# The even mixer's seven input units run on activations times scale, with the root applied to their outputs

## The chip, the core and the metric

The kernel runs on one NeuronCore of a Trainium2 chip. Its engines are TensorE (matmuls; PE in the profile), VectorE (DVE), ScalarE (ACT), GpSimd (POOL) and SyncE (SP), which here only issues transfers. SBUF is the working memory; PSUM has 8 banks of 512 float32 columns, written by TensorE. The metric is the device time of one execution in microseconds (us). Before the change it was 1384.68 us, the median of three runs (1384.54 to 1387.13).

## The reference, cut to what matters

One step of a two-layer trunk over 384 tokens: 128 context tokens and 256 latent ones, 1024 channels, each with its own shift, scale and gate per sub-layer. A layer is feed-forward, mixer, feed-forward. Each sub-layer reads a modulated RMS norm:

```python
def modulate(x, g, shift, scale):
    return rms_norm(x, g) * (1 + scale) + shift

def even_mixer(h, w_in, w_out, ...):
    q, k, v, a = jnp.split(h @ w_in, [ATT_Q, ATT_Q + ATT_KV, ATT_Q + 2 * ATT_KV], axis=-1)
    q = rms_norm(q.reshape(bsz, length, N_HEADS, HEAD_DIM), q_g)
    k = rms_norm(k.reshape(bsz, length, N_KV_HEADS, HEAD_DIM), k_g)
    ...                                   # latent tokens: rotary; cached keys and values put ahead
    glu = a[..., :CONV_CH] * jax.nn.sigmoid(a[..., CONV_CH:])
    conv = jax.nn.silu(layer_norm(depthwise_conv(glu, conv_w, conv_b), cn_g, cn_b))   # 31 taps, 512 channels
    return jnp.concatenate([attn, conv], axis=-1) @ w_out
```

The projection h @ w_in has 14 column tiles of 128: 4 of queries, 1 of keys, 1 of values, 4 + 4 of the gated product.

## The kernel before, in words

Activations lie with channels on the partitions and tokens along the free dimension: x is 8 tiles of 128 channels by 384 tokens. All big products are made in three parts, high and low halves of weights and activations (three(), lines 1417 to 1421). A weight unit is 128 x 2048 float32, two column tiles over 8 row tiles; SyncE loads it (L416) into one of four slots when the unit four places before is done, ScalarE makes its high half (split, L594), VectorE the low one (split, L904), and TensorE runs its 48 matmuls (in_unit). Each engine's order is the order of its block in the file; semaphores tie them.

The mixer has 7 input units: unit 0 is the first pair of gated-product tiles, unit 1 keys and values, 2 and 3 the queries, 4 to 6 the other gated-product pairs; then 4 output units. Ahead of it come feed-forward 0's last unit, whose 8 output tiles VectorE adds to x one by one (L963). ScalarE squares each (L610), TensorE sums over channels and spreads the inverse root to all partitions (norm_sums, norm_spread, with dummy matmuls, L1527, between), VectorE and ScalarE make the scaled, shifted high and low parts (L982, L620, L990), and first_unit follows them tile by tile.

The other boundaries, into the two feed-forwards behind and into the odd mixer, work differently (raw_boundary, raw_norm, raw_units): TensorE multiplies x times scale (xt_hi, xt_lo) with two further columns that hold the shifts, 386 in all, at once for two units, the sums and the spread of the root stand inside, and the outputs are multiplied by the root (n_rms) and get the shift's product added when they are read.

In the mixer, VectorE also has the convolution of channel tiles 0 and 2, one instruction per tap (taps, L1182, 399 columns); tiles 1 and 3 go to TensorE as 8 "quads" each (conv_quads_of, L1716), from copies that SyncE makes by 16 small transfers a tile (L504) as soon as the gated product of that tile is in padded (glu_mul, L1193). The gated product of tile j needs ScalarE's sigmoid j. ScalarE evicts keys, values and queries from PSUM (qkv_evict); VectorE rotates (L1225 to L1234).

The attention has 12 steps m, a pair of heads and 128 tokens each. In step m TensorE runs the scores of m+2, its quads, the values of m-1 and the transposes (flip) of m; ScalarE the exp of m and copies; VectorE a reciprocal (L1260), a scaling (L1265), the maxima of m+1 (L1253) and some taps. After it come the output units, with the convolution's layer norm beside them.

## Time and profile before

| | |
|---|---|
| median of 3 runs | 1384.68 us |
| profiled execution | 1386.83 us, its span 1385.0 us |
| TensorE matmul busy | 1368.4 us, 99% |
| VectorE busy | 972.3 us, 70% |
| ScalarE busy | 552.5 us, 40% |
| GpSimd busy | 47.8 us, 3% |
| mean granted TensorE clock | 0.995 |

The span is from the first to the last instruction of the profiled execution; times in rows are us from its start. A matmul of 384 columns shows 0.34 us although a new one goes out every 0.17, since their ends overlap: the distance between starts is what counts. A value in brackets is the idle time of that engine before the instruction and who ended it. The granted clock is 1.00 at 2.4 GHz and 0.50 at 1.2 GHz.

### The profile page before, as it was taken

To read this page: it belongs to the slowest core of one execution; us is meant where nothing else is said; L and a number is where in the kernel's file an instruction comes from. 1 tells how busy PE (TensorE), PEld (TensorE's weight loads), DVE (VectorE), ACT (ScalarE), POOL (GpSimd) and SP (SyncE) were. 2 spreads that over 40 slices of the span, in tenths; PEclk is the share of its full clock that TensorE was granted. 3 is DMA by queue.
4 is the path that set the end of the run, shared out by engine and by line. 5 is a ranking of instruction groups with operands and counts; after the bars stand their busy time and mean duration, and the time that the engine had idled before them with its cause. 6 is when DMAs were issued, how large, how long until landed. Compare 5 with 4: busy or idle time off the path is not lost.

```text
span 1385.0 us, 21119 instructions
## 1 busy us (share of the span) xinstructions
PE 1368.4 (99%) x8065; PEld 1331.5 (96%) x8065; DVE 972.3 (70%) x1474; ACT 552.5 (40%) x758; POOL 47.8 (3%) x50
## 2 busy tenths in 40 slices
PE   7999999999999999999999999999999999999999
PEld 6999999999948999999999999999998999999999
DVE  5698889948885988888339888888386588443522
ACT  4433333235476643333226433332274463333320
POOL 0000000011001200000002000000020100000000
PEclk8999999999999999999999999999999999999999
DMA  9766567533411465564334666665334253333331
...
DMA packets 48758, 245.65 MB, mean 177 GB/s; under 512 B 6336, under 2 KB 10688, under 8 KB 28096
## 3 DMA queue, kind: packets, MB, share of 16 engines
...
q8 instruction: 34, 0.56, 0.2%
q14 instruction: 20, 0.16, 0.0%
q10 hardware_dynamic: 288, 0.13, 0.0%
HBM read 240.80 MB, written 1.70 MB: 175 GB/s over the span
## 4 chain that ended last, share of the span: by engine, by line
PE 96%; DVE 2%; DMA 1%; ACT 1%; SPq 0%; issue 0%; DVEq 0%; ACTq 0%
PE ps L1419 30%; PE ps L1421 30%; PE ps L1420 30%; DMA m_raw<-in_w_pairs 1%; PE ps L1825 1%; PE ps L1827 1%; PE ps L1826 1%; PE ps L1480 0%; DVE conv L1182 0%; PE ps L1754 0%; PE ps L1496 0%; PE ps L1716 0%; PE ps L1728 0%; DVE smax L1253 0%; PE ps L1854 0%; PE ps L1743 0%
## 5 line engine op out<-in xcount | busy, mean ns | idle before, releaser
L1419 PE MATMUL ps<-a_hi,w_hi 128*128 128x384 f32 x1552 | 522.3, 337 | 0.5 <-DVE a_lo L990 0.3
L1420 PE MATMUL ps<-a_lo,w_hi 128*128 128x384 f32 x1552 | 519.3, 335 | 0.0
L1421 PE MATMUL ps<-a_hi,w_lo 128*128 128x384 f32 x1552 | 519.2, 335 | 0.0
L904 DVE TENSOR_TENSOR w_lo<-w_raw,w_hi 128x2048 fp32r<-128x2048 f32 x153 | 352.0, 2302 | 176.9 <-ACT w_hi L594 176.8
L594 ACT ACTIVATE w_hi<-w_raw 128x2048 fp32r<-128x2048 f32 x153 | 291.7, 1910 | 247.3 <-DMA w_raw<-in_w_units 247.1
L926 DVE SCALAR_TENSOR_TENSOR m_raw<-m_raw 128x1024 f32<-128x1024 f32 x256 | 299.2, 1218 | 0.0
L1419 PEld LDWEIGHTS ps<-a_hi,w_hi 128*128 128x128 f32 x1552 | 291.8, 188 | 6.6 <-issue 3.4
L1420 PEld LDWEIGHTS ps<-a_lo,w_hi 128*128 128x128 f32 x1552 | 291.9, 188 | 0.1
L1421 PEld LDWEIGHTS ps<-a_hi,w_lo 128*128 128x128 f32 x1552 | 291.8, 188 | 0.0
L1421 PE MATMUL ps<-h_hi,w_lo 128*128 (+1 forms) x704 | 235.2, 334 | 0.0
L1419 PE MATMUL ps<-h_hi,w_hi 128*128 (+1 forms) x704 | 235.2, 334 | 0.0
L1420 PE MATMUL ps<-h_lo,w_hi 128*128 (+1 forms) x704 | 235.2, 334 | 0.0
L673 ACT ACTIVATE glu<-ps 128x384 f32<-128x384 f32 x82 | 40.0, 488 | 279.9 <-PE ps L1421 279.9
L1419 PEld LDWEIGHTS ps<-h_hi,w_hi 128*128 128x128 f32 x704 | 132.1, 188 | 0.0
L1420 PEld LDWEIGHTS ps<-h_lo,w_hi 128*128 128x128 f32 x704 | 132.1, 188 | 0.0
L1421 PEld LDWEIGHTS ps<-h_hi,w_lo 128*128 128x128 f32 x704 | 132.1, 188 | 0.0
L1069 DVE TENSOR_TENSOR glu<-glu,ps 128x384 f32<-128x384 f32 x82 | 45.0, 549 | 75.0 <-ACT glu L673 75.0
L675 ACT ACTIVATE h_hi<-glu 128x384 f32 (+1 forms) x82 | 43.1, 525 | 132.6 <-DVE glu L1069 132.6
L1072 DVE TENSOR_TENSOR h_lo<-glu,h_hi 128x384 f32 (+1 forms) x82 | 45.8, 558 | 66.5 <-ACT h_hi L675 66.5
L620 ACT ACTIVATE a_hi<-n_full,m_shift 128x128 fp32r<-128x128 f32 x96 | 42.3, 455 | 45.2 <-DVE n_full L982 45.2
L963 DVE SCALAR_TENSOR_TENSOR x<-ps,m_gate,x 128x128 f32<-128x128 f32 x96 | 34.7, 412 | 26.5 <-PE ps L1421 26.2
L1419 PE MATMUL ps<-xt_hi,w_hi 128*128 128x386 f32 x128 | 44.2, 345 | 0.1
...
## 6 DMA issues: line engine op xcount, KB each, us to landing
...
m_raw<-in_w_rows SPq DMA_DIRECT2D x128, 512.0 KB, 5.5
...
```

What stands on the lines that cost most here:

```text
L594: nc.scalar.activation(w_hi[:, slot(u), :], w_raw[:, slot(u), :], ACT.Copy).then_inc(hi_done, 1)
L620: nc.scalar.activation(a_hi[:, d, lo:hi], n_full[:, d, lo:hi], ACT.Identity, bias=m_shift[:, n, d, cnd:cnd + 1]).then_inc(a_hi_done, 1)
L673: nc.scalar.activation(glu[:, 0, :], ps[:, 2 * b, 0:TOK], ACT.Silu).then_inc(silu_done, 1)
L675: nc.scalar.activation(h_hi[:, bass.ds(t + RING * i, 1), :], glu[:], ACT.Copy).then_inc(h_hi_done, 1)
L904: nc.vector.tensor_tensor(w_lo[:, slot(u), :], w_raw[:, slot(u), :], w_hi[:, slot(u), :].bitcast(FP32), ALU.subtract).then_inc(lo_done, 1)
L926: nc.vector.scalar_tensor_tensor(out, mod_rows(n % TRING), 1.0, cond_row(cnd), ALU.mult, ALU.mult, accum_out=mod_cols[:, bass.ds(FIRST_TIL ...
L963: ins = nc.vector.scalar_tensor_tensor(x[:, d, lo:hi], ps[:, d, lo:hi], m_gate[:, s, d, cnd:cnd + 1], x[:, d, lo:hi], ALU.mult, ALU.add)
L1069: nc.vector.tensor_tensor(glu[:, 0, :], glu[:, 0, :], ps[:, 2 * b + 1, 0:TOK], ALU.mult).then_inc(prod_done, 1)
L1072: nc.vector.tensor_tensor(h_lo[:, bass.ds(t + RING * i, 1), :], glu[:], h_hi[:, bass.ds(t + RING * i, 1), :].bitcast(FP32), ALU.subtract). ...
L1419: mm(out, whi, mhi, start=start, stop=False)
L1420: mm(out, whi, mlo, start=False, stop=False)
L1421: return mm(out, wlo, mhi, start=False, stop=stop)
```

## The change

The mixer's seven input units take the form of the other boundaries. Units 0 and 1 run as raw_units on x times scale, held in a_hi and a_lo (widened to 400 columns); units 2 to 6 read the same 386 columns with in_unit. There is no normed copy of x for the mixer any more, and norm_sums, norm_spread with the dummies, and first_unit are gone. VectorE has a new step take(n) per unit: it copies the shift columns out of PSUM, for keys and queries also times their gain, and multiplies both tiles of the unit (768 columns) by n_rms into SBUF; TensorE may use those banks again after it (in_scaled). ScalarE then works from SBUF with the shift as bias, in two pieces (context and latent tokens) where it had one. The units use banks 0, 2, 4, 0, 2, 4, 2. The transpose of the new keys moves into unit 6. Tile 0's taps are spread anew; all of tile 2's taps stand in the attention's steps, 3 each in steps 0 to 8 and 2 in steps 9 and 10, where 7 stood ahead and then 3, 3, 3, seven times 2, and 1. The first quads go ahead of the second scores. VectorE's split of unit 8 stands behind the attention.

```diff
+    return (a_hi, a_lo) if n == 1 else (xt_hi, xt_lo)
+def glu_pair(j):
+    return prob_t if j % 2 else prob
...
-    norm(1)
+    raw_norm(1, UNIT0[1])
     u = UNIT0[1]
     def sigmoid(n, j):
-        act.wait_ge(unit_done, RING + u + n + 1)
+        act.wait_ge(in_scaled, n + 1)
         if j >= 2:
             act.wait_ge(glu_done, j - 1)
-        nc.scalar.activation(e_sig[:, j % 2, :], ps[:, GLU_BANK[j] + 1, 0:TOK], ACT.Sigmoid).then_inc(sig_done, 1)
+        for cnd, lo, hi in SEGS:
+            ins = nc.scalar.activation(e_sig[:, j % 2, lo:hi], glu_pair(j)[:, 1, lo:hi], ACT.Sigmoid,
+                                       bias=in_shift[:, n, 1, cnd:cnd + 1])
+        ins.then_inc(sig_done, 1)
...
-        act.wait_ge(unit_done, RING + u + n + 1)
+        act.wait_ge(in_scaled, n + 1)
         for h in range(2):
-            m = 2 * (n - 1) + h
-            tile = (QT, None, 0, 1, 2, 3)[m]
-            dst = v_raw[:] if tile is None else qk[:, tile, :]
-            src = ps[:, QKV_BANK[n] + h, 0:TOK]
-            if tile is not None:
-                nc.scalar.activation(qk_sq[:, tile, :], src, ACT.Square).then_inc(qk_sq_done, 1)
-            if tile is None:
-                nc.scalar.activation(dst, src, ACT.Copy).then_inc(qk_copied, 1)
-            else:
-                col = B_KG if tile == QT else B_QG
-                nc.scalar.activation(dst, src, ACT.Copy, scale=vec_b[:, col:col + 1]).then_inc(qk_copied, 1)
-    split(u + 2)
-    split(u + 3)
+            tile = (QT, QT + 1, 0, 1, 2, 3)[2 * (n - 1) + h]
+            if tile <= QT:
+                for cnd, lo, hi in SEGS:
+                    ins = nc.scalar.activation(qk_sq[:, tile, lo:hi], qk[:, tile, lo:hi], ACT.Square,
+                                               bias=in_shift[:, n, h, cnd:cnd + 1])
+                ins.then_inc(qk_sq_done, 1)
+            col = B_KG if tile == QT else B_QG
+            for cnd, lo, hi in SEGS:
+                if tile > QT:
+                    ins = nc.scalar.activation(qk[:, tile, lo:hi], qk[:, tile, lo:hi], ACT.Identity,
+                                               bias=in_shift[:, n, h, cnd:cnd + 1])
+                else:
+                    ins = nc.scalar.activation(qk[:, tile, lo:hi], qk[:, tile, lo:hi], ACT.Identity,
+                                               bias=in_shift_g[:, n - 1, h, cnd:cnd + 1], scale=vec_b[:, col:col + 1])
+            ins.then_inc(qk_copied, 1)
     sigmoid(0, 0)
     split(u + 4)
     qkv_evict(1)
...
-    inverse_rms(1)
-    norm(1)
     u = UNIT0[1]
     tap_at = {}
+    def take(n):
+        bank = IN_BANK[n]
+        dve.wait_ge(unit_done, RING + u + n + 1)
+        dve.wait_ge(rms_copied, 1)
+        shifts = ps[:, bank:bank + 2, TOK:TOK + 2]
+        nc.vector.tensor_copy(in_shift[:, n], shifts)
+        if n in QKV_UNITS:
+            col = B_KG if n == 1 else B_QG
+            nc.vector.tensor_scalar(in_shift_g[:, n - 1], shifts, vec_b[:, col:col + 1], None, ALU.mult)
+            dst = qk[:, (QT, 0, 2)[n - 1]:(QT, 0, 2)[n - 1] + 2, :]
+        else:
+            dst = glu_pair(GLU_UNIT.index(n))[:]
+        nc.vector.tensor_tensor(dst, ps[:, bank:bank + 2, 0:TOK], n_rms[:].unsqueeze(1).to_broadcast([P, 2, TOK]),
+                                ALU.mult).then_inc(in_scaled, 1)
     def taps(j, k0, k1):
...
                 ins.then_inc(conv_done, 1)
     def glu_mul(j):
+        n = GLU_UNIT[j]
+        dve.wait_ge(in_scaled, n + 1)
         dve.wait_ge(sig_done, j + 1)
         dve.wait_ge(e_zero, 1)
         for sgm, lo, hi in SEGS:
-            ins = nc.vector.tensor_tensor(padded[:, j, PAD_AT[sgm]:PAD_AT[sgm] + hi - lo],
-                                          e_sig[:, j % 2, lo:hi], ps[:, GLU_BANK[j], lo:hi], ALU.mult)
+            ins = nc.vector.scalar_tensor_tensor(padded[:, j, PAD_AT[sgm]:PAD_AT[sgm] + hi - lo],
+                                                 glu_pair(j)[:, 0, lo:hi], in_shift[:, n, 0, sgm:sgm + 1],
+                                                 e_sig[:, j % 2, lo:hi], ALU.add, ALU.mult)
         ins.then_inc(glu_done, 1)
     split(u + 2)
-    glu_mul(0)
     split(u + 3)
     dve.wait_ge(vectors_in, 48)
+    take(0)
+    take(1)
+    split(u + 4)
+    glu_mul(0)
     dve.wait_ge(glu_done, 1)
     taps(0, 0, 5)
-    split(u + 4)
-    taps(0, 5, 16)
+    take(2)
     split(u + 5)
-    taps(0, 16, 24)
+    taps(0, 5, 13)
+    take(3)
     split(u + 6)
-    taps(0, 24, 28)
+    taps(0, 13, 20)
     NS = 2 * TT * (QT + 1)
     dve.wait_ge(qk_stat, 1)
     nc.vector.tensor_scalar(stat[:, 0:NS], ps[:, 6, 0:NS], 1.0 / HD, RMS_EPS, ALU.mult, ALU.add).then_inc(qk_ms, 1)
-    taps(0, 28, 30)
+    taps(0, 20, 23)
     dve.wait_ge(qk_root, 1)
     dve.wait_ge(dve_self, mark(nc.vector.reciprocal(stat_row[:, 0:NS], stat_row[:, 0:NS])))
     nc.vector.tensor_copy(qk_wide[:], stat_row[:, 2 * TT * QT:NS].unsqueeze(2).to_broadcast([P, 2 * TT, HD])
                           ).then_inc(qk_wide_done, 1)
-    taps(0, 30, CONV_K)
+    taps(0, 23, 25)
+    take(4)
     split(u + 7)
     glu_mul(1)
     dve.wait_ge(glu_done, 2)
...
     dve.wait_ge(qk_bc, 1)
     dve.wait_ge(roped, 1)
     nc.vector.tensor_tensor(qk[:, QT, :], qk[:, QT, :], ps[:, BC_BANK_K, 0:TOK], ALU.mult).then_inc(k_roped, 1)
+    take(5)
+    taps(0, 25, 28)
     glu_mul(2)
+    taps(0, 28, CONV_K)
     def attention(m):
         width = CTX if m % TT == 0 else LAT + PAST
...
     def mix_low(j, src):
         dve.wait_ge(mix_hi, j + 1)
-        nc.vector.tensor_tensor(a_lo[:, j, :], src, a_hi[:, j, :].bitcast(FP32), ALU.subtract).then_inc(mix_ready, 1)
-    split(u + 8)
-    dve.wait_ge(glu_done, 3)
-    taps(2, 0, 7)
+        nc.vector.tensor_tensor(a_lo[:, j, 0:TOK], src, a_hi[:, j, 0:TOK].bitcast(FP32), ALU.subtract).then_inc(mix_ready, 1)
+    take(6)
+    attention(0)
     glu_mul(3)
-    attention(0)
     attention(1)
     dve.wait_ge(glu_done, CT)
     for m in range(PAIR_STEPS):
...
             mix_low((m - 4) // TT, ps[:, 0, 0:TOK])
         if 1 <= m < PAIR_STEPS - 1:
             attention(m + 1)
-        k = 7 + 2 * m + min(m, 3)
-        taps(2, min(k, CONV_K), min(k + 2 + (m < 3), CONV_K))
+        k = 2 * m + min(m, 9)
+        taps(2, min(k, CONV_K), min(k + 2 + (m < 9), CONV_K))
         if m == PAIR_STEPS - 2:
             dve.wait_ge(conv_done, DVE_TILES)
             a = mark(nc.vector.tensor_tensor(conv_sum(), conv[:, 0, :], conv[:, 2, :], ALU.add))
...
     dve.wait_ge(quad_out, 2)
     nc.vector.tensor_tensor(conv_sum(), conv_sum(), conv[:, 3, :], ALU.add).then_inc(conv_summed, 1)
     mix_low(QT - 1, ps[:, 0, 0:TOK])
+    split(u + 8)
...
     ffn(0)
-    norm(1)
     u = UNIT0[1]
-    first_unit(u, GLU_BANK[0], 1)
-    in_unit(u + 1, QKV_BANK[1])
-    in_unit(u + 2, QKV_BANK[2])
+    raw_units(u, 1)
+    in_unit(u + 2, IN_BANK[2], cols=TOK + 2)
...
         ins.then_inc(qk_bc, 1)
     pe.wait_ge(e_zero, 4)
+    pe.wait_ge(in_scaled, 1)
     qk_sums(QT)
     cached_and_values()
-    pe.wait_ge(glu_done, 1)
-    in_unit(u + 3, QKV_BANK[3])
+    in_unit(u + 3, IN_BANK[3], cols=TOK + 2)
     qk_sums(0)
     qk_sums(1)
-    in_unit(u + 4, GLU_BANK[1], 0, {3: last_sums})
-    in_unit(u + 5, GLU_BANK[2], 0, {3: spread_keys})
-    pe.wait_ge(k_roped, 1)
-    pe.wait_ge(glu_done, 2)
-    nc.tensor.transpose(ps[:, 3, 0:P], qk[:, QT, 0:CTX], ident[:]).then_inc(e_t, 1)
+    pe.wait_ge(in_scaled, 2)
+    in_unit(u + 4, IN_BANK[4], 0, {6: last_sums}, cols=TOK + 2)
+    pe.wait_ge(in_scaled, 3)
+    in_unit(u + 5, IN_BANK[5], 0, {3: spread_keys}, cols=TOK + 2)
+    def keys_out():
+        pe.wait_ge(k_roped, 1)
+        nc.tensor.transpose(ps[:, 0, 0:P], qk[:, QT, 0:CTX], ident[:]).then_inc(e_t, 1)
+    pe.wait_ge(in_scaled, 5)
+    in_unit(u + 6, IN_BANK[6], 0, {6: keys_out}, cols=TOK + 2)
     pe.wait_ge(qk_ms, 1)
-    in_unit(u + 6, GLU_BANK[3])
     pe.wait_ge(glu_done, 3)
     pe.wait_ge(roped, 1)
...
         ins.then_inc(pv_done, 1)
     scores(0)
+    conv_quads_of(QUADS_AT[0])
+    pe.wait_ge(in_scaled, 7)
     scores(1)
-    conv_quads_of(QUADS_AT[0])
     for m in range(PAIR_STEPS):
...
 DFT_BANK = [2, 0, 3]
-GLU_BANK = [0, 2, 4, 6]
-QKV_BANK = {1: 2, 2: 4, 3: 0}
+IN_BANK = [0, 2, 4, 0, 2, 4, 2]
+GLU_UNIT, QKV_UNITS = [0, 4, 5, 6], (1, 2, 3)
 BC_BANK_K = 7
```

VectorE, from unit 4's split (the first row) on; padded is the gated product, conv the taps, w_lo a split. Before:

```order
L904 TENSOR_TENSOR w_lo<-w_raw,w_hi 128x2048
L1182 SCALAR_TENSOR_TENSOR conv<-padded,conv_wt,conv 128x399 x11
L904 TENSOR_TENSOR w_lo<-w_raw,w_hi 128x2048
L1182 SCALAR_TENSOR_TENSOR conv<-padded,conv_wt,conv 128x399 x8
L904 TENSOR_TENSOR w_lo<-w_raw,w_hi 128x2048
L1182 SCALAR_TENSOR_TENSOR conv<-padded,conv_wt,conv 128x399 x4
L1212 TENSOR_SCALAR stat<-ps 128x30
L1182 SCALAR_TENSOR_TENSOR conv<-padded,conv_wt,conv 128x399 x2
L1215 RECIPROCAL stat_row<-stat_row 128x30
```

and now, from the same split:

```order
L909 TENSOR_TENSOR w_lo<-w_raw,w_hi 128x2048
L1206 SCALAR_TENSOR_TENSOR padded<-prob,in_shift,e_sig 128x128
L1206 SCALAR_TENSOR_TENSOR padded<-prob,in_shift,e_sig 128x256
L1189 TENSOR_SCALAR conv<-padded,conv_wt,vec_b 128x399
L1193 SCALAR_TENSOR_TENSOR conv<-padded,conv_wt,conv 128x399 x4
L1175 COPY in_shift<-ps 128x4
L1178 TENSOR_SCALAR in_shift_g<-ps,vec_b 128x4
L1182 TENSOR_TENSOR qk<-ps,n_rms 128x768
L909 TENSOR_TENSOR w_lo<-w_raw,w_hi 128x2048
L1193 SCALAR_TENSOR_TENSOR conv<-padded,conv_wt,conv 128x399 x8
L1175 COPY in_shift<-ps 128x4
L1178 TENSOR_SCALAR in_shift_g<-ps,vec_b 128x4
```

The first gated product and its first five taps now come behind that split, and a take (in_shift, in_shift_g, qk<-ps,n_rms) stands ahead of each further one.

VectorE, from the second gated product on, before (rot and qk<-m_raw are the rotation, L1245 the product that ends the keys):

```order
L1193 TENSOR_TENSOR padded<-e_sig,ps 128x128
L1193 TENSOR_TENSOR padded<-e_sig,ps 128x256
L1225 TENSOR_TENSOR rot<-qk,rope 128x1280
L1230 TENSOR_TENSOR qk<-m_raw,rope 128x5x256
L1234 TENSOR_TENSOR qk<-qk,rot 128x5x256
L1245 TENSOR_TENSOR qk<-qk,ps 128x384
L1193 TENSOR_TENSOR padded<-e_sig,ps 128x128
L1193 TENSOR_TENSOR padded<-e_sig,ps 128x256
L904 TENSOR_TENSOR w_lo<-w_raw,w_hi 128x2048
L1178 TENSOR_SCALAR conv<-padded,conv_wt,vec_b 128x399
L1182 SCALAR_TENSOR_TENSOR conv<-padded,conv_wt,conv 128x399 x6
```

and now, from the take of unit 5, behind the same keys' product, to the first scores' maxima:

```order
L1175 COPY in_shift<-ps 128x4
L1182 TENSOR_TENSOR prob<-ps,n_rms 128x768
L1193 SCALAR_TENSOR_TENSOR conv<-padded,conv_wt,conv 128x399 x3
L1206 SCALAR_TENSOR_TENSOR padded<-prob,in_shift,e_sig 128x128
L1206 SCALAR_TENSOR_TENSOR padded<-prob,in_shift,e_sig 128x256
L1193 SCALAR_TENSOR_TENSOR conv<-padded,conv_wt,conv 128x399 x3
L1175 COPY in_shift<-ps 128x4
L1182 TENSOR_TENSOR prob_t<-ps,n_rms 128x768
L1274 TENSOR_REDUCE smax<-ps 128x2
L1276 SCALAR_TENSOR_TENSOR smaxn<-smax,stat_row 128x2
L1206 SCALAR_TENSOR_TENSOR padded<-prob_t,in_shift,e_sig 128x128
L1206 SCALAR_TENSOR_TENSOR padded<-prob_t,in_shift,e_sig 128x256
```

Two takes are new; the split has gone from here, and tile 0's last six taps stand where tile 2's first seven did.

TensorE, from the last matmul of unit 6 into the attention (L1728 scores, L1716 quads), before:

```order
L1421 MATMUL ps<-a_hi,w_lo 128x384
L1728 MATMUL ps<-kdup,qk 128x128 x2
L1728 MATMUL ps<-kdup,qk 128x384 x2
L1716 MATMUL ps<-m_raw 32x399 x16
L1728 MATMUL ps<-kdup,qk 128x384 x2
L1716 MATMUL ps<-m_raw 32x399 x4
L1743 MATMUL ps<-ident,prob 128x128 x2
L1728 MATMUL ps<-kdup,qk 128x128 x2
```

and now (L1725 scores, L1713 quads):

```order
L1441 MATMUL ps<-a_hi,w_lo 128x386
L1725 MATMUL ps<-kdup,qk 128x128 x2
L1713 MATMUL ps<-m_raw 32x399 x16
L1725 MATMUL ps<-kdup,qk 128x384 x4
L1713 MATMUL ps<-m_raw 32x399 x4
L1740 MATMUL ps<-ident,prob 128x128 x2
L1725 MATMUL ps<-kdup,qk 128x128 x2
```

The 16 quad matmuls now stand between the first scores and the second.

## Rows read from the trace of the kernel before

**Rows 1.** TensorE in order of time: start, duration, line, operation, tiles, forms, [idle before <-releaser].
```profile
308.42 0.34 PE L1421 MATMUL ps<-h_hi,w_lo 128*128 128x384 f32 x1
...
315.48 0.42 PE L1419 MATMUL ps<-a_hi,w_hi 128*128 128x384 f32 x1
```

**Rows 2.** Windows: stretch, length, each engine's busy us, granted clock, DMA share, GB/s.
```profile
311.90:315.20 3.30, 3.30 (x15) 3.30 (x16) 1.70 (x5) 0.91 (x2) 0.00 (x0) 0.50 0.28 117
18.30:28.40 10.10, 8.89 (x51) 6.25 (x52) 7.19 (x17) 3.71 (x5) 0.00 (x0) 0.50 1.02 422
395.00:400.00 5.00, 2.98 (x24) 1.63 (x26) 4.29 (x12) 4.49 (x14) 0.00 (x0) 1.00 0.00 2
```

**Rows 3.** TensorE in order of time, between the second and third feed-forward.
```profile
734.89 0.34 PE L1419 MATMUL ps<-xt_hi,w_hi 128*128 128x386 f32 x1
...
739.10 0.75 PE L1496 MATMUL ps<-ones,n_acc 128*128 128x1 f32 x6
...
753.14 0.34 PE L1419 MATMUL ps<-a_hi,w_hi 128*128 128x384 f32 x1
```

**Rows 4.** TensorE in order of time: after the third input unit, and at the attention.
```profile
342.46 0.72 PE L1661 MATMUL ps<-pick_half,qk_sq 128*128 128x2 f32 x6
...
380.50 1.14 PE L1728 MATMUL ps<-kdup,qk 64*128 64x128 f32 x8
381.57 2.89 PE L1716 MATMUL ps<-m_raw 128*32 128x399 f32 x32
```

**Rows 5.** VectorE in order of time, even mixer and (last) the third feed-forward.
```profile
345.83 2.28 DVE L904 TENSOR_TENSOR w_lo<-w_raw,w_hi 128x2048 fp32r<-128x2048 f32 x1
348.03 5.32 DVE L1182 SCALAR_TENSOR_TENSOR conv<-padded,conv_wt,conv 128x399 f32<-128x399 f32 x8
...
363.65 0.62 DVE L1193 TENSOR_TENSOR padded<-e_sig,ps 128x128 f32<-128x128 f32 x2 [0.82 <-ACT e_sig L719]
...
368.95 0.55 DVE L1245 TENSOR_TENSOR qk<-qk,ps 128x384 f32<-128x384 f32 x1
...
757.70 1.01 DVE L1048 TENSOR_TENSOR n_sq<-ps,n_rms 128x384 f32<-128x384 f32 x2
```

**Rows 6.** ScalarE in order of time.
```profile
318.63 0.90 ACT L620 ACTIVATE a_hi<-n_full,m_shift 128x128 fp32r<-128x128 f32 x2 [0.41 <-DVE n_full L982]
...
330.73 1.92 ACT L594 ACTIVATE w_hi<-w_raw 128x2048 fp32r<-128x2048 f32 x1 [1.86 <-DMA w_raw<-in_w_units]
```

**Rows 7.** SyncE in order of time, and landing of the issues of L504, 360 to 380.
```profile
364.30 11.32 SPq L504 DMA_DIRECT2D m_raw<-padded  x16
...
DMA to landing us min/median/max: 1.9/2.2/4.0
```

**Rows 8.** VectorE in order of time, attention.
```profile
383.60 0.17 DVE L1260 RECIPROCAL srec<-ssum 128x2 f32<-128x2 f32 x1 [0.25 <-ACT prob L801]
...
386.42 0.95 DVE L1253 TENSOR_REDUCE smax<-ps 128x2 f32<-128x768 f32 x1
...
405.26 0.17 DVE L1260 RECIPROCAL srec<-ssum 128x2 f32<-128x2 f32 x1 [1.25 <-ACT e_sig L801]
...
409.12 0.17 DVE L1260 RECIPROCAL srec<-ssum 128x2 f32<-128x2 f32 x1 [0.27 <-ACT prob L801]
...
414.74 0.17 DVE L1260 RECIPROCAL srec<-ssum 128x2 f32<-128x2 f32 x1 [0.58 <-ACT prob L801]
...
418.80 0.16 DVE L1260 RECIPROCAL srec<-ssum 128x2 f32<-128x2 f32 x1
```

**Rows 9.** Chain of waits: start, duration, work on the chain.
```profile
420.26 0.49 PE ps L1743 x3
...
421.76 0.88 PE ps L1754 x12
...
434.03 0.56 PE ps L1790 x6
```

**Rows 10.** GpSimd in order of time.
```profile
427.58 5.18 POOL L571 TENSOR_TENSOR qk_sq<-qk_sq 128x384 f32<-128x384 f32 x3 [96.34 <-ACT qk_sq L822]
```

162 lines of the change are left out of this document (65 added, 97 removed).

## The prediction

> **What bounds the kernel now.** I read the page's first part, then TensorE's rows in order of time at the start of the even mixer, then the windows with the granted clock, and last VectorE's, ScalarE's and SyncE's rows beside them. TensorE is busy 99% of the span (the table above), so a change pays only where TensorE has no full-size matmul to do. In the part that is edited there are two such places.
>
> The first is the seam between the first feed-forward and the mixer. The last of its matmuls is issued at 308.42, the next full one at 315.48 [rows 1]; between them stand sums, a root, a spread and dummies, all serial. I take the end of the feed-forward as 308.6. The third input unit is done by 342.46, where the small sums start [rows 4], so three units and the seam take 33.9 us. The granted clock is 0.50 from 311.9 to 315.2, the 1.2 GHz level [rows 2]; its cost is part of the 33.9.
>
> The second is the attention. It starts with the scores at 380.50 [rows 4] and ends with the last value products, at 421.76 plus 0.88 [rows 9]. Its twelve steps are a relay of VectorE (maxima, reciprocals, taps of the convolution), ScalarE (exp) and TensorE. VectorE is nearly full: it idles only 0.27 us before three of its reciprocals (the one at 409.12 stands for them), 1.25 before that at 405.26 and 0.58 before that at 414.74 [rows 8]. What is added to VectorE here is therefore mostly paid.
>
> **The seam.** The new form runs units 0 and 1 on x times scale, with the root taken meanwhile. The same code already stands between the second and third feed-forward: its first matmul is at 734.89, and the next kind begins at 753.14, 18.25 us for two units with sums and spread inside, and no wait [rows 3]. The residual additions ahead of it run at the same distance from the seam in both places, and the parameters are ready before them, so I take 18.25 here too: units 0 and 1 end at 308.6 + 18.25 = 326.85. A matmul of 386 columns goes out every 0.175 us (24 of them from 734.89 to 739.10) [rows 3], a unit is 48 of them, 8.4 us. Unit 2 ends at 335.3 instead of 342.5: 7.2 us earlier. Vector work for the norm (32 scaled and low parts) goes, 16 raw low parts come, none of it late.
>
> **Units 3 to 6.** Before, from 342.46 to 380.50 it is 38.0 us of units and small matmuls without a wait [rows 4]. Two columns in 384 add 0.5%, 0.2 us. New waits could stand in it. Values must be copied before their transposes: VectorE takes unit 1 by about 328.2, ScalarE splits unit 4 at 330.73 as before [rows 6] (its load is released by unit 0 in both, at about 326) and is done 332.65, then three pairs of activations of 0.8 to 0.9 each [rows 6] end at 335.2, and TensorE arrives at 335.9. The transpose of the new keys needs the roped keys; they come 5.9 us after the second gated product starts (363.65 to 369.50) [rows 5], in the new order at about 368.4, and TensorE is at its place in unit 6 at 371. I charge nothing; each cover is 0.7 us or more. The units end at 335.3 + 38.2 = 373.5, 7.0 us earlier.
>
> **Where it is given back: the quads' transfers.** The second convolution tile goes by 16 small transfers to TensorE. They are issued on SyncE after the second gated product (glu_done 2), and before took 364.30 to 375.62 to issue, the last started 10.7 after the first and landing a median 2.2 later [rows 7]. Before, TensorE reached the quads at 381.57 [rows 4] and never felt them. When is that product ready now? VectorE's program from ScalarE's 332.65 on: four splits of 2.20 (345.83 to 348.03), 25 taps of 0.655 (eight are 5.3 us) = 16.3, two gated products of 0.65 [rows 5], three statistics operations 0.75 together, and three new "take" steps. A take reads two banks, 768 columns, times the root, and copies the shifts. No row has it: from below 0.5 (the 384-column one, two in 1.01 [rows 5]), from above two such, 1.1 with the copies; a pitch of 0.46 for 384 columns makes 768 nearer the upper end, and I take 1.0 to 1.1. Together 8.8 + 16.3 + 1.3 + 0.75 + 3.2 = 30.35: the product is ready at 363.0, only 1.3 earlier than before. VectorE stays the pace although TensorE gained 7: it stands idle from about 328.2 to 332.65, and then does the same taps and more. The last transfer starts at 373.7 and lands at 375.9.
>
> The new TensorE order is scores(0), four quads (2.9 us [rows 4]), scores(1). Scores(0) is done at 374.0; TensorE stands until 375.9, the quads end at 378.8, scores(1) 0.85 later, and VectorE's maximum over 768 columns and its scaling (0.95 and 0.1 [rows 8]) at 381.0. Take 6, which sits behind three taps and ends at 375.1, is covered by that; so is ScalarE's last sigmoid with the table load, which leave exp(0) at 378.2. The first reciprocal now stands behind the second maximum, at 381.1; before it was at 383.60 [rows 8]. So 2.5 us remain of the 7.0.
>
> **The taps in the attention.** All 31 taps of the other vector tile now stand in the steps; before 7 of them were done ahead. Steps 0 to 2 keep three taps; steps 3 to 8 get a third one, step 10 a second: 7 x 0.655 = 4.6 us. The idle time that can take them is 3 x 0.27 + 1.25 + 0.58 = 2.6 [rows 8], so the last reciprocal is about 1.9 us later relative to the start. The last reciprocal has some 0.9 us to spare: it and its scaling are over at 419.4 (418.80 and 0.6 [rows 8]), and the flips that need them are released by other work and run at 420.26 [rows 9]. So 1.1 us reaches the end. Bounds: 0 (all hidden) and 4.6 (none).
>
> **After it.** The split of unit 8 moves from before the attention to its end, 2.2 us ahead of the layer norm, which waits for TensorE's means anyway, so it starts only some 0.65 later. GpSimd's three additions follow, 427.58 to 432.76 [rows 10], and TensorE uses them at 434.03 [rows 9], so 0.65 still fits. Everything later keeps its distance.
>
> **Sum.** -2.5 + 1.1 = -1.4 us. The profiled execution is 1386.83 us (span 1385.0 and 1.8 around it) and would become 1385.4; it lies 2.15 above the median of the runs, 1384.68, and the runs' time becomes 1383.3.
>
> **Rivals.** (a) The transfers don't hold TensorE: they issue faster (without the long issues among them) and the product is ready sooner. For it: nothing in the trace ever waited for them. Against it: 11.3 us for 16 is what stands there [rows 7]. Then the start is bounded by take 6 at 375.1, exp(0) at 378.2 and the second maximum, first reciprocal at 378.4, 5.2 earlier: -5.2 + 1.1 = -4.1, 1380.6. Halfway is possible. (b) The taps are paid in full, because a later maximum delays exp, the flips and the next maximum in turn: -2.5 + 4.6 = +2.1, 1386.8. For it: in steps 0 to 3, which have three taps already, the chain of waits runs through VectorE alone. Against it: from step 5 to 10 it runs through TensorE and ScalarE. (c) Slower: TensorE's clock. The new stand of 1.9 us before the quads has no instruction in it. The clock fell to 1.2 GHz at 18.3, after a thin stretch from 14.6, and at 311.9, after the 3.3 us since the last full matmul; it stayed low for 10.1 us and for 3.3 [rows 2]. If it falls at about 376 for 10 us, the quads and scores(1) cost 3.65 us more and two steps of some 3 us of TensorE work lose about a microsecond each: -1.4 + 5 = +3.6, 1388.3. It decides from the point where the transfers land so late that the stand resembles the stretches ahead of those two falls; I reckon it shorter. Against it: in 395 to 400 TensorE was busy 2.98 of 5 us and the clock stayed at 1.00 [rows 2]. ("TensorE: Matmul & The Clock Gate" of the Trainium skill, section on the HAM clock gate, says that idling brings half the clock and that activity releases it; by that rule the old seam's fall belongs to what the change removes, and the trace agrees with the 0.50 in it, and the new stand is where it could return.)
>
> **Chances.** Forecast 0.48, (a) or most of it 0.28, (b) 0.13, (c) 0.11. Its own range is 1381.8 to 1385.0 (product and landing 0.8 either way, taps 0 to 2). To hold 8 in 10 I reach down past (a) to 1379.8 and up to (b) at 1386.8. A measurement tells 0.2% (2.8 us) from no change: faster, below 1381.9, is (a) and a sixth of the forecast, 0.36; slower, above 1387.5, is (c) and a part of (b), 0.14; the rest 0.50.
>
> **What will show it.** In the changed profile: no small matmuls between feed-forward and mixer, 18.2 us for units 0 and 1, clock 1.00; the units ending near 373.5; 16 transfers from 363; a stand of about 2 us of TensorE before the quads, released by a transfer; first reciprocal at 381; VectorE without idle time in steps 3 to 8; attention ending about 421.2 instead of 422.6. The forecast is wrong if TensorE's quads start straight behind scores(0), if a unit waits for a take, or if the clock falls in the attention.

## Result and profile after

The changed kernel takes 1391.09 us (median of 12 runs, 1388.05 to 1394.51), the kernel before, beside it, 1385.18 (12 runs, 1384.36 to 1388.84): ratio 1.0037, 95% interval 1.0029 to 1.0044. It is 5.1 us slower by the ratio and 5.9 by the medians. The forecast was 1383.3, with 1386.8 as the upper end. The profiled executions differ by 4.8: 1391.61 us with a span of 1389.8, against 1385.0 (the table of before). What follows accounts for these 4.8.

The seam went as forecast, and so did most of the mixer. TensorE in order of time in the changed kernel; the rows answer [rows 1, 4, 9] and, from 464 on, the start of the sums (ones, n_acc) and of the spread (ident, stat) at the next boundaries:

```profile
309.05 0.33 PE L1441 MATMUL ps<-h_hi,w_lo 128*128 128x384 f32 x1
309.23 0.34 PE L1439 MATMUL ps<-a_hi,w_hi 128*128 128x386 f32 x1
...
313.44 0.75 PE L1506 MATMUL ps<-ones,n_acc 128*128 128x1 f32 x6
...
335.93 0.72 PE L1654 MATMUL ps<-pick_half,qk_sq 128*128 128x2 f32 x6
...
374.34 0.49 PE L1725 MATMUL ps<-kdup,qk 64*128 64x128 f32 x4
376.69 4.58 PE L1713 MATMUL ps<-m_raw 128*32 128x399 f32 x32 [1.85 <-DMA m_raw<-padded]
381.20 1.56 PE L1725 MATMUL ps<-kdup,qk 64*128 64x384 f32 x8
...
422.21 0.88 PE L1751 MATMUL ps<-prob_t,v_nat 128*64 128x128 f32 x12 [0.69 <-ACT prob_t L796]
...
437.20 0.83 PE L1796 MATMUL ps<-e_diag,ones 128*128 128x128 f32 x6
...
464.34 0.83 PE L1506 MATMUL ps<-ones,n_acc 128*128 128x1 f32 x6 [1.02 <-POOL n_acc L550]
...
467.24 0.83 PE L1479 MATMUL ps<-ident,stat 128*128 128x128 f32 x6
...
741.34 0.83 PE L1506 MATMUL ps<-ones,n_acc 128*128 128x1 f32 x6
```

The mixer's first matmul follows the feed-forward's last one by 0.18 us, where there were 7 us before. The small sums behind unit 2 come at 335.93 instead of 342.46, the attention at 374.34 instead of 380.50. Then the quads stand 1.85 us for their transfers and take 4.58 us instead of 2.89. The attention ends at 422.21 + 0.88, where it ended at 421.76 + 0.88 before. The feed-forward ahead of the mixer ends at 309.2 in this profile, not at 308.6; against that offset of 0.6 the mixer up to the attention's end is 0.15 us faster and no more.

The granted clock at the quads, in windows (columns as in [rows 2]):

```profile
376.00:377.00 1.00, 0.31 (x4) 0.16 (x8) 0.56 (x3) 0.88 (x3) 0.00 (x0) 0.92 0.72 134
377.00:380.00 3.00, 3.00 (x24) 0.96 (x20) 0.75 (x2) 2.28 (x6) 0.00 (x0) 0.50 0.96 380
380.00:381.00 1.00, 1.00 (x16) 0.26 (x8) 0.00 (x0) 0.00 (x0) 0.00 (x0) 0.88 0.98 377
```

A clock of 0.92 in the first window, 0.50 in the second and 0.88 in the third make 3.4 us at 1.2 GHz. The fall comes just behind the stand, and the quads take 1.7 us longer by it. VectorE, answering [rows 5, 8]:

```profile
333.99 2.29 DVE L909 TENSOR_TENSOR w_lo<-w_raw,w_hi 128x2048 fp32r<-128x2048 f32 x1 [4.88 <-ACT w_hi L600]
...
363.39 0.74 DVE L1206 SCALAR_TENSOR_TENSOR padded<-prob_t,in_shift,e_sig 128x128 f32<-128x128 f32 x2
...
375.12 0.95 DVE L1182 TENSOR_TENSOR prob_t<-ps,n_rms 128x768 f32<-128x768 f32 x1
...
382.16 0.96 DVE L1274 TENSOR_REDUCE smax<-ps 128x2 f32<-128x768 f32 x1 [4.42 <-PE ps L1725]
...
383.23 0.17 DVE L1281 RECIPROCAL srec<-ssum 128x2 f32<-128x2 f32 x1
...
419.79 0.16 DVE L1281 RECIPROCAL srec<-ssum 128x2 f32<-128x2 f32 x1
```

VectorE stands 4.88 us for unit 4's split (it waits for ScalarE's half) and 4.42 for the second scores. The second gated product ends at 364.1 (forecast 363.0), the 16 transfers go out from 364.16 to 375.24 (before 364.30 to 375.62 [rows 7]).

The loss lies behind the mixer, and a little of it ahead. In the table are stage lengths, each the difference of two row starts as above; "end of mixer" is from the last small matmuls of the layer norm (e_diag) to the sums of the next boundary, the others from a spread to the next sums, the last to the end of the span. With the tiles 384 columns apart such a stage repeats to 0.1 us from profile to profile of the same program. With 400 columns the odd mixer does not: it takes 93.07 to 93.14 us in three of the six profiles that have it, this one among them, and 92.65 in the other three. The 0.45 us lie among the last 24 matmuls ahead of the next sums, and what decides on them is not shown. The second feed-forward has 0.2 us more here than in the other five (273.89 to 273.90).

| us | before | after | difference |
|---|---|---|---|
| start to the end of the first feed-forward | 308.6 | 309.2 | +0.6 |
| from there to e_diag | 128.0 | 128.0 | 0.0 |
| end of mixer | 26.21 | 27.14 | +0.93 |
| second feed-forward | 273.37 | 274.10 | +0.73 |
| third | 273.58 | 273.89 | +0.31 |
| odd mixer | 91.49 | 93.14 | +1.65 |
| fourth | 272.35 | 272.93 | +0.58 |

These sum to 4.8 us, the difference of the spans (the four boundaries' own 2.8 to 2.9 us each differ by 0.1 at most). No instruction of the last four rows computes anything else than before. Two things around them are different: the tiles of a_hi and a_lo lie 400 columns apart, and the program ahead has other instructions and another number of them.

### The profile page after: what moved, and what is told of

Its sections match the earlier page's. It is cut to its first block, busy times and chain, and to the rows that moved or that the text cites. A ratio compares the mean times of both kernels' runs of the same rounds, so it can differ in the third digit from the quotient of the medians.

```text
span 1389.8 us, 21090 instructions
## 1 busy us (share of the span) xinstructions
PE 1369.2 (99%) x8037; PEld 1332.0 (96%) x8037; DVE 977.0 (70%) x1476; ACT 556.2 (40%) x774; POOL 49.5 (4%) x52
## 4 chain that ended last, share of the span: by engine, by line
PE 67%; DVE 3%; issue 2%; SPq 1%; POOL 1%; ACT 0%; DMA 0%; DVEq 0%; POOLq 0%; ACTq 0%
PE ps L1439 21%; PE ps L1441 21%; PE ps L1440 21%; DVE conv L1193 1%; PE ps L1824 1%; PE ps L1823 1%; PE ps L1825 1%; SPq L511 1%; DVE smax L1274 1%; POOL n_acc L550 1%; PE ps L1713 0%; PE ps L1852 0%; PE ps L1506 0%; PE ps L1843 0%; PE ps L1479 0%
## 5 line engine op out<-in xcount | busy, mean ns | idle before, releaser
L1439 PE MATMUL ps<-a_hi,w_hi 128*128 128x384 f32 (+1 forms) x1552 | 524.7, 338 | 0.1
L1440 PE MATMUL ps<-a_lo,w_hi 128*128 128x384 f32 (+1 forms) x1552 | 521.9, 336 | 0.0
L1441 PE MATMUL ps<-a_hi,w_lo 128*128 128x384 f32 (+1 forms) x1552 | 521.8, 336 | 0.0
L619 ACT ACTIVATE a_hi<-n_full,m_shift 128x128 fp32r<-128x128 f32 x80 | 35.4, 455 | 39.7 <-DVE n_full L987 39.6
```

The costliest lines, as they stand in the source:

```text
L619: nc.scalar.activation(a_hi[:, d, lo:hi], n_full[:, d, lo:hi], ACT.Identity, bias=m_shift[:, n, d, cnd:cnd + 1]).then_inc(a_hi_done, 1)
L1439: mm(out, whi, mhi, start=start, stop=False)
L1440: mm(out, whi, mlo, start=False, stop=False)
L1441: return mm(out, wlo, mhi, start=False, stop=stop)
```

## Experiments

Each time measured below is the median of 5 to 12 executions, and its ratio is to the kernel before, run beside it, whose median lay between 1385.68 and 1386.12. The kernels' code is shortened below. A trace is one execution, up to 2.6 us from its kernel's median.

**The distance of the tiles.** First the kernel before with wide tiles of which it reads the same 384 columns (XT_N is 400):

```diff
-a_hi = sb("a_hi", [P, KT, TOK], F32R)        # and a_lo
+a_hi = sb("a_hi", [P, KT, XT_N], F32R)[:, :, 0:TOK]
```

> The kernel before, with one edit: the tiles of a_hi and a_lo lie 400 columns apart in SBUF instead of 384; every instruction reads and writes the same 384 columns as before. Theory W (the distance of the tiles): the changed kernel's matmuls on a_hi and a_lo are issued irregularly and about 0.0005 us further apart in the feed-forwards (0.1733 before, 0.1738 to 0.1739 after), 0.005 in the odd mixer's row units; over some 4,600 of the first and 150 of the second that is 2.3 + 0.8 = 3 us: 1388.2, ratio 1.002. Theory R (the place): all that lies behind a_lo has moved by 1024 bytes, and that is what counts: also 1388.2. Theory T (timing alone: what is lost after the mixer comes from loads and additions that start later, not from the layout): 1385.2, ratio 1.000, and an unchanged distance of the matmuls.

Measured: 1389.6 us, ratio 1.0028 (1.0017 to 1.0038). Then the kernel before with unused memory behind the two tiles instead:

```diff
 a_lo = sb("a_lo", [P, KT, TOK], F32R)
+sb("a_room", [P, 2 * KT * (XT_N - TOK)], F32R)
```

> The kernel before, with one edit: 1024 unused bytes per partition behind a_lo, so that all that lies behind it has the address of the changed kernel, while the tiles of a_hi and a_lo stay 384 columns apart. Theory W: no change, 1385.2. Theory R: 1388.2, as with the wide tiles. Theory T: no change, 1385.2.

Measured: 1386.23, ratio 1.0002 (0.9993 to 1.0011). TensorE's spread and the next sums around the second feed-forward and around the odd mixer, first with the wide tiles, then with the room:

```profile
467.96 0.83 PE L1470 MATMUL ps<-ident,stat 128*128 128x128 f32 x6
...
741.85 0.75 PE L1497 MATMUL ps<-ones,n_acc 128*128 128x1 f32 x6
...
1021.65 0.83 PE L1470 MATMUL ps<-ident,stat 128*128 128x128 f32 x6
...
1114.72 0.73 PE L1497 MATMUL ps<-ones,n_acc 128*128 128x1 f32 x6
```

```profile
465.78 0.83 PE L1470 MATMUL ps<-ident,stat 128*128 128x128 f32 x6
...
739.14 0.75 PE L1497 MATMUL ps<-ones,n_acc 128*128 128x1 f32 x6
...
1018.43 0.83 PE L1470 MATMUL ps<-ident,stat 128*128 128x128 f32 x6
...
1109.93 0.72 PE L1497 MATMUL ps<-ones,n_acc 128*128 128x1 f32 x6
```

273.89 and 93.07 us against 273.36 and 91.50. The same instructions on the same data take 0.5 us more per feed-forward and 1.6 in the odd mixer (0.4 of them are the wait named above, so 1.2 for the matmuls), only because the tiles are further apart; moving what lies behind them by 1024 bytes costs nothing that the interval can show. Theory W stands, R and T fall. The first feed-forward, whose start differs from profile to profile, says the same behind it: from 86.04 us (its 201st matmul that reads a_hi) to 217.08 (the first that reads h_hi) it is 131.04 us before, and so in all seven profiles with tiles 384 apart; in all six with 400 it is 131.47. What follows there reads h_hi and h_lo, whose tiles have not moved, and takes 91.35 in both. In the changed kernel the wide form is needed only by the seven input units, so the rest can keep its own view of the same memory:

```diff
+a_hi, a_lo = first KT * TOK columns of each, as [P, KT, TOK]     # feed-forwards, output units, odd mixer
+xa_hi, xa_lo = all KT * XT_N columns, as [P, KT, XT_N]           # raw_pair(1), in_unit with 386 columns
```

(in words, not code)

> The changed kernel, with one edit: the seven input units still read 386 columns of tiles 400 apart, but everything else (feed-forwards, output units, odd mixer) lays its tiles 384 apart in the same memory. Addresses behind a_lo are those of the changed kernel. Theory W: 3 us less than the changed kernel, 1388.1, ratio to the kernel before 1.002; what then remains of the 5.9 us is the mixer and its seam to the third sub-layer (1.5 us in the traces). Theory R or T: as the changed kernel, 1391.1, ratio 1.004.

Measured: 1387.88, ratio 1.0020 (1.0010 to 1.0030), and in its trace the feed-forwards are 273.47, 273.37 and 272.45 us, the odd mixer 91.49: what the distance costs is back in these stages. The ratio gains only 0.0017, 2.4 us, since its profile loses 1.4 us elsewhere, at the boundary ahead of the second feed-forward (under "The instruction fetch").

Two more runs ask what it is about the distance that costs, both in the kernel before:

```diff
+sb("a_shift", [P, 16], F32R)
 a_hi, a_lo as before                    # distance 384, begin 64 bytes later
```

> The kernel before, with one edit: a_hi and a_lo begin 64 bytes later, their tiles still 384 columns (1536 bytes) apart; what lies behind them is 1024 bytes later as in the run with the room, which cost nothing. It asks what about the distance of 1600 bytes costs. Theory A (where a tile begins: 1600 bytes put every second tile on an address that is no multiple of 128 bytes, and here all are): the cost is there in full or double, 1389 to 1393, and the matmuls on a_hi show 337 to 339 ns instead of 336. Rival D (the distance itself, not where a tile begins): 1386, and 336, 334, 334 ns as before.

```diff
-a_hi = sb("a_hi", [P, KT, TOK], F32R)        # and a_lo
+a_hi = sb("a_hi", [P, KT, 416], F32R)[:, :, 0:TOK]     # 1664 bytes, 13 x 128
```

> The kernel before, with one edit: the tiles of a_hi and a_lo are 416 columns (1664 bytes, 13 x 128) apart, 32 unused columns in each where the distance of 400 has 16. Theory A (a tile that begins off a multiple of 128 bytes costs): no cost, 1386, 336, 334, 334 ns. Rival D (any distance other than that of the tiles' own width costs) : 1389 to 1390, as with 400. A finer rule, with multiples of 256 or 512 bytes wanted, would also show a cost here and in part of the tiles.

Measured: with the shift 1387.02, ratio 1.0007 (0.9998 to 1.0016); with 416 1394.53, ratio 1.0064 (1.0050 to 1.0077). By stages:

| us | second, third feed-forward | odd mixer | of it a_hi, a_lo stationary | moving | fourth |
|---|---|---|---|---|---|
| 384 | 273.37, 273.58 | 91.49 | 32.90 | 33.31 | 272.35 |
| 384, 64 bytes later | 273.38, 273.60 | 92.38 | 33.81 | 33.29 | 272.45 |
| 400 | 273.89, 274.09 | 93.07 | 33.60 | 33.78 | 272.88 |
| 416 | 274.97, 275.19 | 92.61 | 33.60 | 33.71 | 274.00 |

A matmul holds one operand, the stationary one, and runs the other, the moving one, through it. The two new columns are from the first to the last start of the odd mixer's 144 matmuls with a_hi or a_lo as the stationary operand (in pieces of 128 columns) and of its 192 with them as the moving one. In the feed-forwards they are the moving operand.

Theory A fails where it was meant: in the feed-forwards the shift costs nothing and 416 costs three times what 400 does, 1.6 us each, though no tile's begin has moved against a multiple of 128 bytes. There the distance itself counts; rival D had the kind right, but gave 416 the price of 400. With the tiles as the stationary operand it is otherwise: the shift alone costs 0.9, and 400 and 416 cost 0.7 each. Why a matmul is issued later when its neighbour tile is further away no run shows.

**The order at the attention's start.**

```diff
 scores(0)
-conv_quads_of(QUADS_AT[0])
 pe.wait_ge(in_scaled, 7)
 scores(1)
+conv_quads_of(QUADS_AT[0])
```

> The changed kernel, with one edit: the second scores stand ahead of the first quads again, as before the change. The unit's outputs are taken at 376.1 in the changed kernel's trace, so the second scores can go there; the second maximum then starts at about 378 instead of 382.2, the first reciprocal at 379 instead of 383.2. Theory V (VectorE sets the pace of the steps, and the stand of TensorE ahead of the quads was the loss): the attention ends 3 to 4 us earlier, 1387.5. Theory Q (the four quads only move into the relay: they run at half clock behind the second scores and delay the third scores and the first flip): gain 0 to 1, 1390.5.

Measured: 1388.41, ratio 1.0022 (1.0010 to 1.0034), 2.1 us better than the changed kernel by the ratios, where theory V had 3 to 4. Its executions lie between 1385.74 and 1393.99, and the profiled one, 1387.12, is among the faster. VectorE there (the first scores start 0.5 earlier than in the changed kernel's profile):

```profile
377.25 0.95 DVE L1274 TENSOR_REDUCE smax<-ps 128x2 f32<-128x768 f32 x1
...
378.98 0.17 DVE L1281 RECIPROCAL srec<-ssum 128x2 f32<-128x2 f32 x1 [0.58 <-ACT prob L806]
```

The first reciprocal is 4.25 us earlier and the attention ends at 417.96 instead of 422.21, just as much: 3.8 us without the offset. The 16 quad matmuls, now behind 0.92 us of scores, take 2.89, so a part of the 3.8 is the clock, at most the 1.7 that the quads had lost, and the rest is the order. Theory V stands in the trace.

**The stand and the clock.** Nine dummy matmuls (2.27 us), whose results nobody reads, in the place of the stand, in the changed kernel:

```diff
 scores(0)
+for _ in range(9):
+    mm(ps[:, IDLE_BANK, 0:128], ones[:], ident[:, 0:128], start=True, stop=True)
 conv_quads_of(QUADS_AT[0])
```

> The changed kernel, with one edit: nine dummy matmuls (128 x 128, 36 instructions) between the first scores and the first quads, where TensorE stood 1.85 us for the quads' transfers. Theory C (the stand itself costs the clock): the granted clock stays 1.00 from 376 to 381, the 16 quad matmuls take 2.9 us instead of 4.58, the first reciprocal and the end of the attention come 1.7 us earlier. Rival: the clock falls all the same, since the thin stretch is longer than the stand, and nothing changes there. Theory F (instruction fetch): the q8 packet of 16 KB, one per some 256 TensorE instructions, lay 2.5 us behind the issue of a weight load in the changed kernel (444.75 against 442.28) and 0.6 us ahead of it in the kernel before (441.0 against 441.68), and the load took 5.9 us instead of 4.6; 36 instructions more put the fetch 3 us earlier, the load takes 4.7 again, and TensorE's wait of 1.0 us for GpSimd's sums ahead of the third sub-layer is gone. C and F together: -2.7 us, 1388.4; C alone -1.7, F alone -1.0.

Measured: 1389.89, ratio 1.0031 (1.0022 to 1.0040): 0.8 us better by the ratios, where both theories together have 2.7, and not told apart from none by the intervals. The profiled execution, 1387.78, is among the faster, and the slower ones have a lower mean clock (0.994 at 1392 and 1393 us, 0.997 in the profiled one), so the clock fell somewhere in them too; where, no profile shows. The profiled one is plain on both theories.

```profile
373.81 2.27 PE L1758 MATMUL ps<-ident,ones 128*128 128x128 f32 x18
376.01 2.89 PE L1713 MATMUL ps<-m_raw 128*32 128x399 f32 x32
```

The granted clock is 1.00 throughout, the quads take 2.89 instead of 4.58, and from the first scores to the second maximum it is 6.4 us instead of 7.8. So the stand itself had brought the clock down: the granted clock fell at the quads in the three profiles with a stand of 1.82 us or more there and in none of the others. Part is given back ahead of it: in this trace TensorE waits 0.77 us for ScalarE's copies of the values, since unit 4's load lands 6.5 us behind its issue, not 5.4 (more on that load below).

**The instruction fetch.** What made the end of the mixer 0.93 us longer? ScalarE's third split there waits for its load in the changed kernel and does not in the kernel before:

```profile
448.24 1.92 ACT L600 ACTIVATE w_hi<-w_raw 128x2048 fp32r<-128x2048 f32 x1 [1.17 <-DMA w_raw<-in_w_units]
```

That load of 1 MB is issued at 442.28 and lands 5.9 us later; before it was issued at 441.68 and took 4.6. Nothing else is loaded then, but for one packet of 16 KB on the queue for instructions (q8). Such packets come every 15 to 23 us in the mixer; inside each feed-forward there is a stretch of 153 to 158 us without one. Nine dummies of 16 columns in the opening, far ahead, move it:

```diff
 keep_busy(BUSY_OPENING)
+for _ in range(9):
+    mm(ps[:, IDLE_BANK, 0:16], ones[:], ident[:, 0:16], start=True, stop=True)
```

> The changed kernel, with one edit: nine dummy matmuls of 16 columns more (36 instructions) in the opening, behind the 22 that stand there, where TensorE waits for parameter loads. This moves only the instruction fetches. Theory F: the load takes 4.7 us instead of 5.9, ScalarE's third split doesn't wait, TensorE's wait of 1.0 us for GpSimd ahead of the third sub-layer is gone, and the kernel is 1.0 us faster, 1390.1, if no other load is hit instead. Rival B (the load is late for another reason, the second set of quad transfers or the later split of unit 8): load 5.9, wait 1.0, 1391.1. The quads' stand and the clock at 376 to 381 stay as they were.

Measured: 1390.1, ratio 1.0025 (1.0014 to 1.0036), 1.7 us better than the changed kernel by the ratios, with overlapping intervals; the trace decides. Queue packets from 444.75 to 445.00 and the load's landing (issue, KB, median us) in the changed kernel:

```profile
q8 instruction: 1, 0.02, 23.5%
...
w_raw<-in_w_units SPq DMA_DIRECT2D x1, 1024.0 KB, 5.9
```

With the dummies in the opening, packets from 441.75 to 442.00, and the same load, issued at 442.26:

```profile
q8 instruction: 1, 0.02, 29.9%
...
w_raw<-in_w_units SPq DMA_DIRECT2D x1, 1024.0 KB, 4.7
```

The packet came 2.5 us behind the issue and comes 0.4 ahead of it now. The load is back at 4.7 us, TensorE's wait for GpSimd is gone, and the end of the mixer takes 26.41 instead of 27.14 (the 0.2 that remains is the distance: the wide kernel before has 26.39). Theory F stands, B falls. The packet is TensorE's, since only its instructions were added. All nine profiles of kernels with the change agree: in the five with the changed kernel's count of TensorE instructions the packet comes 2.5 to 3.0 us behind the issue and the load takes 5.9 to 6.1, in the four with nine dummies more it comes at the issue or up to 0.5 ahead of it and the load takes 4.7 to 4.8. How the packet holds the load up isn't shown. In the kernel with the two views the same wait (1.31 us) was followed by a granted clock of 0.57 from 464 to 468, and the boundary took 4.3 us instead of 2.9.

**VectorE's stand ahead of the transfers.** In the changed kernel:

```diff
 sigmoid(0, 0)                    # ScalarE
-split(u + 4)
 qkv_evict(1)
+split(u + 4)
...
 take(1)                          # VectorE
-split(u + 4)
 glu_mul(0)
 taps(0, 0, 5)
+split(u + 4)
```

> The changed kernel, with one edit: unit 4's split goes behind the keys' and values' activations on ScalarE, and behind the first gated product and its five taps on VectorE, which otherwise stands 4.9 us for that split from 329.1 on. It tests the step of the forecast by which the quads' transfers hold TensorE because VectorE stands idle there. Theory S: the second gated product comes some 3 us earlier (360 instead of 363.4), the last transfer lands before the first scores are done, TensorE does not stand ahead of the quads, the granted clock stays 1.00, and with 1.85 us of stand and 1.7 of slow matmuls gone the second maximum starts at about 379 instead of 382.2: 2.5 to 3.5 us faster, 1388. Rival: the time is taken up by the next wait (the take of unit 4 or the sigmoid), and 0 to 1 us is gained.

Measured: 1388.82, ratio 1.0021 (1.0012 to 1.0030), 2.2 us better than the changed kernel by the ratios.

```profile
374.44 0.88 PE L1713 MATMUL ps<-m_raw 128*32 128x399 f32 x8 [1.50 <-DMA m_raw<-padded]
...
377.26 1.56 PE L1725 MATMUL ps<-kdup,qk 64*128 64x384 f32 x8
```

VectorE at the splits of units 4 and 5 and at the second gated product:

```profile
334.08 2.29 DVE L909 TENSOR_TENSOR w_lo<-w_raw,w_hi 128x2048 fp32r<-128x2048 f32 x1 [3.00 <-ACT w_hi L600]
...
338.84 2.29 DVE L909 TENSOR_TENSOR w_lo<-w_raw,w_hi 128x2048 fp32r<-128x2048 f32 x1 [1.40 <-ACT w_hi L600]
...
361.13 0.74 DVE L1206 SCALAR_TENSOR_TENSOR padded<-prob_t,in_shift,e_sig 128x128 f32<-128x128 f32 x2
```

The sequence starts 1.9 us earlier in this profile (unit 2's sums at 334.04 against 335.93), so the gated product is only 0.4 earlier beside it (361.13 against 363.39), not 3. VectorE did its other work ahead of the split, but stood 3.00 us for unit 4's split and then 1.40 for unit 5's, 4.4 in all where it was 4.88. Unit 4's load landed 7.4 us behind its issue, not 5.4. Unit 5's load, issued 3.5 us behind it, and the two copies of the keys, issued at 328.98 and 329.75 here and at 335.55 and 336.17 in the changed kernel, lie within its time; no run has them apart. The transfers still hold TensorE 1.5 us; yet here the clock did not fall at the quads, and the second maximum is 2.0 us earlier beside the rest. So both were half right: the stand stays, the slow matmuls went.

**Together.** Views and the second scores first:

> The changed kernel with both edits that gained: tiles 384 apart outside the seven input units, and the second scores ahead of the first quads. If the two losses are separate they add: 1.0037 - 0.0017 - 0.0015 = 1.0005, 1386.8. If they hide each other (the later attention lies under nothing, the slower matmuls are spread over the whole kernel, so I don't see how), 1.002. In its trace I expect the 1 MB load behind the fourth output unit's predecessor to land late again (6.0 us instead of 4.7) and TensorE to wait 1 us for GpSimd's sums ahead of the third sub-layer.

Measured: 1384.85, ratio 0.9996 (0.9985 to 1.0006); the sum, 1.0005, lies within the interval; the late load and the wait for GpSimd (1.29 us) are there as expected. With nine dummies of 64 columns between first and second scores:

> The kernel with both edits, and nine dummy matmuls of 64 columns between the first and the second scores, where TensorE would wait 1.4 us for the last take. By theory F the load takes 4.7 us and the wait ahead of the third sub-layer goes (-1.0, and -1.4 more if the clock no longer falls behind that wait), by theory C nothing is lost at the quads: 1386.8 - 1.0 to 2.4 = 1384.4 to 1385.8, ratio 0.999 to 1.000. If neither holds: 1386.8.

Measured: 1382.97, ratio 0.9977 (0.9968 to 0.9986), 2.6 us better than the run before it, where 1.0 to 2.4 were expected; 1.4 us of the difference between the two profiles lie in the attention, where the clock fell in the run before and not here. In its trace: load 4.7 us, no wait for GpSimd, end of mixer 26.20. And with unit 4's split moved as above:

> The kernel with tiles 384 apart outside the input units, the second scores first and nine short dummies ahead of them, and the same new place of unit 4's split. In its trace TensorE waited 0.26 and 0.77 us for the keys' and values' activations behind a late split of unit 4, 1.0 in all, and VectorE's last take came 0.4 us after the unit's end. Expected: these waits go, 1.0 to 1.5 us less than the 1383.0 of that kernel, ratio to the kernel before 0.9967. Rival: the attention's start is set by the last take, the last sigmoid, the table load and the first exp, and nothing is gained there, 0.5 us at most.

Measured: 1381.67, ratio 0.9972 (0.9963 to 0.9981), 3.9 us faster than the kernel before. The step over the run before it is 0.7 us, nearer the rival's 0.5 than the 1.0 to 1.5 expected, and within the intervals. The waits for the keys' and values' activations are gone, but its profile shows the clock falling in the middle of the attention:

```profile
391.00:394.00 3.00, 1.24 (x10) 0.87 (x10) 2.89 (x7) 2.30 (x7) 0.00 (x0) 0.97 0.01 3
394.00:397.00 3.00, 2.95 (x16) 0.94 (x20) 2.86 (x8) 2.24 (x7) 0.00 (x0) 0.50 0.00 0
```

The clock fell once between 393 and 403, where TensorE has little to do, in five of the fourteen profiles (this one, the one with unit 4's split moved alone, the views with the scores first, and the kernels before with 400 and 416 columns), and not in those of the kernel before [rows 2] and the changed one. From the first reciprocal to the end of the mixer's layer norm (e_diag) it is 55.25 to 55.60 us with the fall and 53.84 to 53.99 without, in the profiles of kernels with the change: 1.4 to 1.7 us, which make single profiles differ. What decides on it stays open.

## Why the prediction was wrong

**The seam.** Right: unit 2 over at 335.3 forecast and 335.93 measured, of which 0.6 is the offset. The clock of 1.2 GHz there is gone: its window was 0.50 before [rows 2], the new one shows 1.00 from 311 to 316. But it does not come in every execution: it stands in two of the five profiles with the old seam. With tiles 384 apart the feed-forward's last matmul and the first scores are 72.08 and 72.04 us apart in those two and 71.23 in the third, so some 0.8 of the 7 us gained belong to that fall, and an execution without it has less to give.

**Units 3 to 6.** Right within 0.3: scores at 374.34 against 373.5 plus the offset. The cover of 0.7 us at the values' transposes was as thin as it looked: it held in this profile and failed by 0.58 to 0.77 in four later ones.

**The transfers.** Right in kind and size: 363.0 forecast and 364.1 with 0.6 of offset, a stand of 1.9 forecast and 1.85 measured. The 0.5 us between come from a load that I took over as it was [rows 6]. ScalarE in the changed kernel:

```profile
332.04 1.92 ACT L600 ACTIVATE w_hi<-w_raw 128x2048 fp32r<-128x2048 f32 x1 [3.15 <-DMA w_raw<-in_w_units]
```

Unit 4's load was issued at 326.0 before and landed 4.7 us later; now it is issued at 326.6 and takes 5.4. Units 0 and 1 now end together, so unit 5's load is issued 2.8 us behind it, where it was 8.3. In all nine profiles of kernels with the change unit 5's load follows within 2.0 to 3.9 us and unit 4's takes 5.4 to 7.4; in the five others it follows after 8 us and more and unit 4's takes 4.7 to 4.8. That one load slows the other is argued from this, not tested.

**The clock at the quads.** Wrong. I gave it 0.11 as a rival with 10 us at 1.2 GHz and reckoned the stand too short. It fell for 3.4 us, and cost 1.7. The forecast and rivals (a) and (b), 0.89 together, all had the clock up. (By the section on the HAM clock gate in "TensorE: Matmul & The Clock Gate" of the Trainium skill idling brings the clock down; the trace agrees, with 0.50 behind 1.85 us of it.) The first reciprocal kept 1.0 us of the 7.0, not 2.5; the 1.7 would have made it 2.7.

**The taps in the attention.** From the first to the last reciprocal it is 36.56 us against 35.20 [rows 8], 1.4 more where I had 1.9, and the attention ends 0.8 later against that start, where I had 1.1. Rival (b), paid in full, is out.

**"Everything later keeps its distance."** This is the step that failed, for 4.2 of the 4.8 us; the other 0.6 stand ahead of the mixer. I had read the edit of a_hi and a_lo as one of memory only and priced the two columns more in the units that read them. The declaration of 400 columns touches some 4,300 matmuls outside the mixer; it costs 0.5 us in each of the later feed-forwards, 0.43 of the first one's 0.6, 0.2 at the end of the mixer and 1.2 in the odd one, 3.3 to 3.5 together by these stages. The run that has it alone is 3.9 us slower by its ratio (2.4 to 5.3), and its odd mixer has 0.4 of the wait on top, as the changed kernel's has. Another 0.75 is the fetch: the change has fewer TensorE instructions ahead of that load, so a packet that used to run ahead of it fell into it. Neither was among the rivals, and no row of before has a matmul on the same tile at two distances.

With the sizes put in: -0.15 for the mixer up to the attention's end, +3.4 for the distance, +0.45 for the wait in the odd mixer and +0.75 for the fetch make 4.45. The difference of the spans is 4.8, and 5.1 is that by the ratio; the rest, up to 0.2 at each of several stages, was not looked into. That the measured time is slower, as rival (c) had it, is no merit of that rival: the mixer with its fallen clock is not slower, and the loss is elsewhere.
